# Changing the place of small pieces of work in a decoder trunk: gate rows, sample scores, norms, first blocks and a queue's order

## The reference, cut to what matters

```
mod    = c @ w_ada[l] + b_ada[l]                 # 2 layers x 12 blocks of 512 columns: shift, scale, gate
u      = x * (1 + scale(c)) + shift(c)
# layer 0
q, k, v, mq, mk, mv, og, ig, fg = split(u @ w_in_even)      # "ein": 3072 columns and 8 gate columns
A      = softmax(q k1 - alibi) v - lam * softmax(q k2 - alibi) v     # 4 differential heads, causal; samples: paged past too
M      = mlstm(mq, mk, mv, ig, fg)               # 4 heads; state C, n, m; normalised by max(|den|, exp(-m))
mix    = concat(rms(A) * gA, rms(M) * g * sigmoid(og))
x      = LayerNorm(ALPHA * x + (1 + gate(c)) * (mix @ w_out_even))   # "eout"
x      = LayerNorm(ALPHA * x + (1 + gate(c)) * swiglu(u'))           # ffn 0
# layer 1
xr, g  = u @ w_in_odd                             # "oinx", "oing"
xc     = conv4(xr);  r, i = sigmoid(xc @ w_a), sigmoid(xc @ w_x)     # "wax"
a      = exp(-8 r softplus(-lambda));  h_t = a h_(t-1) + sqrt(1 - a^2) i xc
x      = LayerNorm(ALPHA * x + (1 + gate(c)) * ((gelu(g) * h) @ w_out_odd))   # "oout"
x      = LayerNorm(ALPHA * x + (1 + gate(c)) * swiglu(u'))           # ffn 1
```

## Time and profile before

| | |
|---|---|
| median of 3 runs | 1556.14 us (1552.59 to 1557.97) |
| the profiled execution | 1546.92 us, of it the span 1545.3 us |
| PE busy | 1413.6 us, 91% |
| DVE, ACT, POOL busy | 775.5 us (50%), 529.4 us (34%), 319.1 us (21%) |
| mean bandwidth from and to HBM | 112 GB/s over the span |

### The profile page before, as it was taken

The page is one execution under the profiler, slowest core; times in us unless marked ns, Lnnn a source line. Parts: engine busy times, 40 slices in busy tenths (PEclk is TensorE's granted clock), DMA queues, the critical chain, the costliest instruction groups (busy, mean ns, idle before and its releaser), DMA issues.

```text
span 1545.3 us, 29474 instructions
## 1 busy us (share of the span) xinstructions
PE 1413.6 (91%) x12260; PEld 1353.9 (88%) x12260; DVE 775.5 (50%) x1179; ACT 529.4 (34%) x736; POOL 319.1 (21%) x303
## 2 busy tenths in 40 slices
PE   5799977788697999999999988988989999999996
PEld 4799966665597999999999988988989999999995
DVE  2633248764457633333334687788574333333256
ACT  0311143243323333212223345785433321222224
POOL 2000031021116500000002624634543000000054
PEclk9899988999898999999999999999999999999999
DMA  9522277666813122243322402221513224432211
GB/s 320 180 87 82 83 274 242 215 235 222 281 39 83 55 82 75 76 123 96 97 60 76 137 28 78 92 61 53 162 38 110 65 59 114 129 85 65 76 38 56
DMA packets 213505, 175.08 MB, mean 113 GB/s; under 512 B 9080, under 2 KB 183933, under 8 KB 213253
## 3 DMA queue, kind: packets, MB, share of 16 engines
q1 hardware_dynamic: 208448, 160.13, 33.7%
q0 software_dynamic: 4800, 13.23, 2.5%
q10 hardware_dynamic: 140, 0.09, 0.0%
HBM read 167.87 MB, written 5.63 MB: 112 GB/s over the span
## 4 chain that ended last, share of the span: by engine, by line
PE 53%; DVE 11%; ACT 3%; issue 2%; POOL 0%; ACTq 0%; DVEq 0%; POOLq 0%
PE ps L2647 44%; PE ps L2672 4%; PE ps L2656 3%; DVE gn L2100 2%; DVE wlo L1900 2%; DVE UL L2107 1%; ACT whi L1152 1%; DVE rstd L2073 1%; DVE xc L2221 1%; DVE xc L2255 0%; DVE xc L2256 0%; DVE tv L2065 0%; PE ps L2867 0%; ACT xT L1226 0%; DVE xT L2050 0%
## 5 line engine op out<-in xcount | busy, mean ns | idle before, releaser
L2647 PE MATMUL ps<-UH,whi 128*128 128x260 f32 x1840 | 372.8, 284 | 11.6 <-DVE wlo L1900 8.1
L2647 PE MATMUL ps<-UH,wlo 128*128 128x260 f32 x1840 | 372.6, 284 | 0.0
L2647 PE MATMUL ps<-UL,whi 128*128 128x260 f32 x1840 | 372.2, 284 | 0.0
L1152 ACT ACTIVATE whi<-raw 128x2048 fp32r<-128x2048 f32 (+3 forms) x104 | 178.0, 1712 | 433.2 <-PE ps L2647 396.7
L2647 PEld LDWEIGHTS ps<-UH,whi 128*128 128x128 f32 x1840 | 285.9, 190 | 12.6 <-issue 6.4
L2647 PEld LDWEIGHTS ps<-UH,wlo 128*128 128x128 f32 x1840 | 285.7, 190 | 0.0
L2647 PEld LDWEIGHTS ps<-UL,whi 128*128 128x128 f32 x1840 | 285.0, 190 | 0.0
L1900 DVE TENSOR_TENSOR wlo<-raw,whi 128x2048 fp32r<-128x2048 f32 (+3 forms) x104 | 224.4, 2158 | 79.1 <-ACT whi L1152 78.5
L2154 DVE TENSOR_TENSOR hb<-ps,silb 128x520 f32<-128x520 f32 x44 | 30.8, 700 | 267.4 <-PE ps L2647 247.3
L814 POOL COPY accS<-xT 128x520 f32<-128x520 f32 x4 | 2.5, 622 | 628.2 <-DVE xT L2032 628.2
L2647 PE MATMUL ps<-HH,whi 128*128 128x260 f32 x484 | 97.4, 283 | 0.0
(11 more groups left out here) (493 smaller groups left out, 2546.5 us busy)
## 6 DMA issues: line engine op xcount, KB each, us to landing
raw<-in_w_ada SPq DMA_DIRECT2D x96, 512.0 KB, 6.3
raw<-in_w_ffn_in SPq DMA_DIRECT2D x88, 512.0 KB, 5.0
raw<-in_w_in_even SPq DMA_DIRECT2D x24, 512.0 KB, 4.7
raw<-in_w_ffn_out SPq DMA_DIRECT2D x32, 384.0 KB, 4.0
raw<-in_w_ffn_out SPq DMA_DIRECT2D x32, 320.0 KB, 3.3
raw<-in_w_in_odd SPq DMA_DIRECT2D x20, 512.0 KB, 4.6
raw<-in_w_out_odd SPq DMA_DIRECT2D x16, 320.0 KB, 3.5
page<-in_cache_k POOLq DMA_DIRECT2D x16, 256.0 KB, 4.2
```

The lines of the kernel that those rows point to most:

```text
L1152: ins = nc.scalar.activation(whi[w % 2][:, 0:f], raw[c % NRAW][:, 0:f], ACT.Identity)
L2647: ins = T.matmul(ps(g)[:, hf, 0:HT], wt(k, m), x[:, k, hf], start=(k == 0 and wt is wh and x is xh), stop=(k == s.k - 1 and wt is wl_))
```

## The change: places of work, and orders in queues

Five places change. No matmul of a projection is added or removed.

1. The first four blocks are taken in the order 0, 2, 1, 3; the first chunk of `ein` is loaded between the pairs, and PE does the second pair between the fourth and the fifth k-slice of that chunk. The second pair's turns go to the second bank of the block's own PSUM group.
2. At the gate rows, blocks 4 and 5 are copied before DVE's running sums.
3. In the steps, the pieces for the samples move to later steps.
4. The two high and low halves for `eout` and the norms of heads 0 to 2 move into step 16. The mixing goes in the order `MIXED`, the sample columns of all eight tiles as one piece "S".
5. In the second mixer ACT copies `xrS` and frees the group; the GELUs of tiles 4 and 5 come earlier in ACT's queue, two low halves change their places in DVE's.

The diff follows, cut to its core, engine by engine. The plan and SP:

```diff
-PAST_AT, TURN_AT = {10: 0, 12: 1, 13: 2, 15: 3}, {11: 0, 13: 1, 14: 2, 16: 3}
+PAST_AT, TURN_AT = {11: 0, 12: 1, 14: 2, 15: 3}, {12: 0, 13: 1, 15: 2, 16: 3}
...
+FIRST_BLOCKS = (0, 2, 1, 3)
+MIXED = (0, 1, 2, "S", 4, 5, 6, 3, 7)
...
+    one(("mod", 0), ("mod", 1), ("sel", 0), ("sel", 1), ("mod", 2), ("mod", 3))
     stage("ein", 12, 8, 256, 2)
+    st["ada0"].chunks[4:] = [5, 6, 7, 8]
+    st["ein"].chunks[0] = st["ein"].c0 = 4
...
+                    if s.c0 == 0 and c == NRAW:
+                        load(st["ein"], 0)
```

POOL in the steps:

```diff
                     for e in range(2):
                         load_page(e, "cache_v", e)
+                if s_ == 9:
                     pool.wait_ge(n_new, 1)
...
-                if s_ == 8:
+                if s_ == 10:
                     pool.wait_ge(cgain_ready, 1)
...
-                if s_ in (11, 13, 14):
+                if s_ in (12, 13, 15):
                     p = TURN_AT[s_]
                     wait_filled(pool, use[("pv8", p)])
```

ACT, in the steps, then in the second mixer:

```diff
+                if s_ == 16:
+                    act.wait_ge(tokens_stored, 32)
+                    act.wait_ge(sample_stored, 48)
+                    hi(st["eout"].c0)
+                    hi(st["eout"].c0 + 1)
+                    link(nc.scalar.activation(sml[:, 12:13], epsc[:], ACT.Sqrt))
                 if quarter == 0 and 1 <= h <= H:
                     head_out(h - 1)
...
+                nc.scalar.activation(xrS[:, t].rearrange("p (a b) -> p a b", a=2), ps(g)[:, :, HALF:HT], ACT.Identity)
                 nc.scalar.activation(xc[:, t], pT(g), ACT.Identity, scale=OT[:, t, 35:36],
                                      bias=OT[:, t, 36:37]).then_inc(cv0, 1)
                 settled(act, cv0)
+                free(nc.scalar.activation(sml[0:1, 13:14], ps(g)[0:1, 0, 0:1], ACT.Identity), g)
...
+            gelu(0)
+            gelu(4)
+            gelu(5)
+            gelu(1)
+            gelu(2)
+            high_y(0)
```

DVE at the gate rows, in the steps, in the mixing, in `make_u0` and in the second mixer:

```diff
             link(v.tensor_scalar(rows[0:4, 0], rows[0:4, 0], 15.0, None, ALU.mult))
+            block_rows(FIRST)
+            block_rows(FIRST + 1)
+            block_select(FIRST)
...
+                if s_ == 16:
+                    lo(st["eout"].c0)
+                    wait_filled(dve, use[("pv8", 3)])
+                    lo(st["eout"].c0 + 1)
+                    dve.wait_ge(den_ready, H - 1)
+                    dve.wait_ge(expm_ready, 1)
+                    norm_floor(slice(0, 96))
...
-                if s_ == 0:
+                if s_ == 7:
                     own_scores()
-                if s_ == 3:
                     sample_gates()
-                if s_ == 4:
                     state_dots()
-                if s_ == 5:
+                if s_ == 8:
                     pack_states()
...
+            mixed(0)
+            dve.wait_ge(root_ready, 2)
+            v.reciprocal(R[96:128, 0:P], R[96:128, 0:P])
...
+                    if t == 4:
+                        low(3)
+                    if t % 4 == 0:
+                        first_scale_and_shift(t // 4)
                     if t == 2:
-                        lo(st["ein"].c0)
-                    if t == 5:
-                        lo(st["ein"].c0 + 1)
+                        lo(st["ein"].chunks[0])
...
                 low(KD - 1)
+                lo(st["ein"].chunks[1])
...
-                free(v.tensor_copy(xrS[:, t].rearrange("p (a b) -> p a b", a=2), ps(g)[:, :, HALF:HT]), g)
-                dve.wait_ge(freed[g % NGRP], g // NGRP + 1)
...
                 scan(t)
-                if t == 2:
+                if t == 0:
                     lo(p0 + 12)
```

PE in the mixing and in the first chunk of `ein` and `eout`:

```diff
-            for t in range(8):
+            for i, t in enumerate(MIXED):
                 g = use[("rb", t)]
+                if t == "S":
+                    pe.wait_ge(r_ready, 2)
...
+                ks = [t for t in MIXED if t != "S"] if mixer else list(range(s.k))
+                for i, k in enumerate(ks):
+                    if i == 4 and between is not None:
+                        between()
+                    pe.wait_ge(ready, max(4, i + 2) if mixer else n_ready + k + 1)
...
+                for d in (2, 3):
+                    block_products(d)
+                for d in (2, 3):
+                    block_turn(d)
...
-            gemm("ein", UH, UL, ulo_ready, 0)
+            gemm("ein", UH, UL, ulo_ready, 0, between=last_blocks)
```

More of the change, by code:

```diff
@@ L545, in weight_view @@
                 both = [a["w_ada"][l].rearrange("(e k p) (c m) -> c e p k m", e=2, p=P, m=512) for l in range(2)]
-                return [both[block_of(s, c) // 12][block_of(s, c) % 12][c % 2] for c in range(s.n)]
+                named = [FIRST_BLOCKS[d] if d < FIRST else d for d in range(NBLK)]
+                return [both[named[block_of(s, c)] // 12][named[block_of(s, c)] % 12][c % 2] for c in range(s.n)]
             if n == "ein":
@@ L628, in _ @@
                 turn = s.c0 > 0 and is_ada(s.c0 - 1) != is_ada(s.c0)
-                peel = min(s.n, NRAW) if s.c0 == 0 or turn else 0
+                peel = NRAW + (s.name == "ein") if s.c0 == 0 or turn else 0
                 if is_ada(s.c0) and s.c0 > 0:
                     peel = s.n
-                for c in range(peel):
+                for c in range(s.name == "ein", peel):
                     load(s, c)
@@ L949, in middle_act @@
             settled(act, zeroed)
-            for tb in range(1, 4):
-                token_rows(tb)
+            token_rows(2)
+            token_rows(3)
             for tb in range(4):
@@ L1451, in _, with gelu @@
             s = st["oing"]
-            for t in range(KR):
-                if t == 6:
-                    hi(p0 + 15)
-                if t == 8:
-                    hi(p0 + 16)
+            def gelu(t):
                 g = s.groups[t // 2][t % 2]
@@ L1469, in _ @@
                     act.wait_ge(freed[g % NGRP], g // NGRP + 1)
-                if t >= 1:
-                    high_y(t - 1)
-            high_y(KR - 1)
+            gelu(0)
[4 more added lines that the diff above has]
+            high_y(0)
+            gelu(3)
+            high_y(1)
+            gelu(6)
+            high_y(2)
+            gelu(7)
+            hi(p0 + 15)
+            for t in range(3, 6):
+                high_y(t)
+            gelu(8)
+            high_y(6)
+            high_y(7)
+            gelu(9)
+            hi(p0 + 16)
+            high_y(8)
+            high_y(9)
             s = st["oout"]
@@ L1870, in middle_dve @@
+            dve.wait_ge(mix_hi, 4)
+            v.tensor_tensor(samples(ML[:]), ms, samples(MH[:].bitcast(F32)), ALU.subtract).then_inc(mix_lo, 1)
+            settled(dve, mix_lo)
+            for i in range(5, 9):
+                mixed(i)
+                low_mixed(i - 1)
+            low_mixed(8)
             for j in range(2):
@@ L1959, in block_rows @@
                 wait_filled(dve, g)
+                if d in (2, 3):
+                    v.tensor_copy(modrow[:, d % 2], ps(g)[:, 0, 0:P]).then_inc(rows_copied, 1)
+                    settled(dve, rows_copied)
+                    return
                 free(v.tensor_copy(modrow[:, d % 2], ps(g)[:, 0, 0:P]), g)
@@ L1992, in _, with first_scale_and_shift @@
             setup_dve()
-            for d in range(FIRST):
-                block_rows(d)
-                if d >= 1:
-                    block_select(d - 1)
-            block_select(FIRST - 1)
-            scale_and_shift(0)
+            def first_scale_and_shift(i):
+                for d in (2 * i, 2 * i + 1):
+                    block_rows(d)
+                for d in (2 * i, 2 * i + 1):
+                    block_select(d)
+                t = slice(4 * i, 4 * i + 4)
+                link(v.tensor_scalar(G9[:, 0, t], part(0, 1)[:, t], 1.0, None, ALU.add))
+                link(v.tensor_copy(B9[:, 0, t], part(0, 0)[:, t]))
             def make_u0():
@@ L2665, in first_k_ordered @@
                 pe.wait_ge(lo_done, split_index[s.c0] + 1)
-                for k in range(s.k):
-                    pe.wait_ge(ready, n_ready + k + 1)
+                mixer = s.name == "eout"
+                ks = [t for t in MIXED if t != "S"] if mixer else list(range(s.k))
[3 more added lines that the diff above has]
+                    pe.wait_ge(ready, max(4, i + 2) if mixer else n_ready + k + 1)
                     for m in range(s.uses):
@@ L2823, in block_turn @@
             def block_turn(d):
+                gm = use[("mod", d)]
+                if d in (2, 3):
+                    pe.wait_ge(rows_copied, d - 1)
+                    T.matmul(ps(gm)[:, 1, 0:36], modrow[:, d % 2], cn[:, C_ADA:C_ADA + 36], start=True, stop=True).then_inc(turned, 1)
+                    return
                 g = use[("sel", d)]
                 begin(g)
-                gm = use[("mod", d)]
                 pe.wait_ge(freed[gm % NGRP], gm // NGRP + 1)
```

243 lines of the change are left out of this document (137 added, 106 removed).

## The result

The changed kernel takes 1546.36 us (median of 13 runs, 1544.73 to 1549.52) against 1556.14 us for the kernel before in the same job (13 runs, 1549.53 to 1565.36): a ratio of 0.9933 [0.9913, 0.9953], or 9.8 us. It is faster, as forecast, but by 9.8 instead of 24.2 us. The profiled execution took 1548.51 us.

A forecast was written before the change was run, and what follows sets the result against it. TensorE was busy 1413.6 of 1545.3 us, so only about 132 us could be won from. Terms -7 + 0 - 2.5 - 7.7 - 7 = -24.2, taken off the median 1556.14, gave 1532 us; range 1519 to 1548.

The forecast's parts named there:

- A: Start, first blocks in pairs: the first projection's chunk 1 begins at 56.3 instead of 64.28; taken as 7 us, bounds 4 to 8.5.
- B: Gate rows: the 7.02 us wait for VectorE becomes a wait for DMA; gain 0, from -1.5 to +1.5 us.
- C: The 18 steps: later sample pieces bring early steps forward, little is left at the loop's end; -2.5 us, from -6 to +2.
- The sign that the prediction had named: Loop's end: the forecast is wrong if the loop's last steps come later than today.
- 4.9 us of moved work at nothing: Steps 7 to 9: 4.9 us of moved work costs nothing in VectorE's pauses; 9.4 us falls to about 4.5.
- rival 3: Steps 7 to 14: pushed-together sample pieces each show TensorE a wait of 4.5 us; slower, 1561 us; chance 0.04.
- the pages' "about 10 us": Loop's end: last value pages, asked for after step 14, needed after step 15; issue some 4 us, landing 5.9.
- ACT's halves in an idle time of 7.82 us: Ahead of the last head's outputs: the idle time holds two high halves of 1.91 us and a table load, if chunks landed.
- Rival 2: Loop's end: shared DMA engines make last pages and projection chunks late, holding the last head; about 1540 us; chance 0.14.
- D: Norms and mixing: from last sums to output projection 13.8 us instead of 21.5; gain 7.7, bounds 5 to 10.
- E: Second mixer: xrS waits of 7.7 us and a low-half wait of 4.83 go; -7 us, from -3 to -10.
- rival 1: Second mixer: waits only change hands within VectorE's queue, gain there 1 us; total 1538 us; chance 0.17.

The follow-up runs named there:

- the second pair: pages_early against old_steps, which differ by the moved steps and both keep the halves ahead of the last head: 1552.39 and 1543.77 us.
- the first experiment: The kernel before, unedited, profiled a second time: 1558.41 us, 0.9993 of before, profiled span 1556.9.
- combined_again: combined run once more without edit, beside combined_moved: 1538.44 us, 0.9895 of before.
- combined_moved: Against combined: sample pieces in the change's later steps, third pair of value pages used in step 13: 1546.64 us, 0.9957 of before.
- combined: Changed kernel with sample pieces, pages, state products in before's steps, halves behind the last head, second mixer's projection low half first: 1535.24 us, 0.9858 of before.
- pages_early: Changed kernel with the third pair of value pages used in step 13 instead of 14, the fourth asked for a step earlier: 1552.39 us, 0.9962 of before.
- old_steps: Changed kernel with all sample pieces, pages and state products in before's steps, the rest kept: 1543.77 us, 0.9901 of before.

## Why the prediction was right in direction and wrong in size

**A and B** came out by their mechanism: 5.9 of 7 us at chunk 1, less by DVE's later tiles (1.4) and the slow clock behind PE's new pause (0.7), and at the gate rows the wait for DVE turned into one for a transfer. Together -4.7 at step 0, or -6.5 against the profile from which the forecast was read.

**C is the step that failed**, in both halves: in the table above 8.9 of the 14.2 us by which -10.0 misses -24.2 are C's. The sign that the prediction had named came: the loop ends later than before (last sums at 425.96, 415.78 and 424.29 in the two profiles of before).

*Up to step 13* the prediction said that pieces taken out of the front make Sb earlier, which they do (unit 9 comes 96.9 us after the first Sb, against 102.4 in the quick profile and 107.4 in the other), and that 3.7 us of this would be kept at step 13. It was not shown to be kept: unit 13 comes after 151.0 us, against 144.0 and 153.8. PE's idle time over the steps is 32.4 us after and 31.3 to 31.7 before. The waits of the earlier trace rows were not removed: after, the Sb rows among PE's waits are these (who, whom, us, times, longest):

```profile
PE ps L2501 <- DVE Sb L1591: 9.1, 6, 2.4
...
PE ps L2596 <- DVE Sb L1591: 3.5, 1, 3.5
```

The prediction had priced 4.9 us of moved work at nothing, to lie in DVE's pauses. Its sum there is wrong as well: of the 7.7 us it charged 2.8, so 9.4 falls to 6.6; it took off the 4.9 instead and wrote 4.5. The experiments say that the moves as a whole are worth less than nothing: 8.2 us worse with the end repaired, 8.6 in the second pair. Not quite half of that is idle time in the last units; the rest is clock, and a profile of one execution cannot tell a lower clock that the order causes from one by chance (the first experiment). The clocks of the other runs point the same way, 0.958 to 0.966 in the six runs of combined_again and 0.953 to 0.960 in the eleven of combined_moved. The medians show the sum, and the windows that it is lost behind unit 12. There PE's waits in combined_moved are for `pvrow` (4.6 us, 2.6 in combined), for Sb (2.0, 0.5) and for `proj` of the past values (1.6, none). That points at the values over the past, which are pushed together there much as rival 3 described, at a smaller price; no run moves them alone, and which of the pieces costs it stays open.

*At the end* the prediction took -2.5 for all of C, with +2 as the worst, and this stretch alone measured +7.2. It had seen both mechanisms, and judged that both would just fit. The term that failed in the changed kernel is the pages' "about 10 us" between asking and need. They are asked for from 397.21 on, and PE would have taken the first at 401.49 (403.33 less its wait), 4.3 us later; the four take 4.2, 4.9, 6.5 and 7.9 us to land. PE stands 5.15 us for them, and 1.6 us go to the slow clock behind the wait. The other term, ACT's halves in an idle time of 7.82 us "if the two chunks have landed by then", failed too, since they had not: the first chunk is asked for at 399.19 and split at 408.33. But in the changed kernel this cost nothing, because the head itself came later still; it costs 3.4 to 5.1 us at the end where the pages come early (pages_early, old_steps). Pages and chunks are asked for in the same 5 us, 3 MB in all: the halves of the two chunks take 8.7 us to land (median of four), against 6.7 in the kernel before and 5.2 and 6.0 in the two kernels with early pages. Rival 2 described this lateness. That its price of about 8 us (pages, head, and a part of D) lies near the 7.2 is luck: the pages and the clock behind them cost nearly all of it instead of 2 to 3 us, the head behind ACT cost nothing, and D lost nothing. The rule of the Trainium skill cited beside C, that transfers of all issuing engines share the same 16 DMA engines ("DMA: Bandwidth & Descriptors", section "Issuing engines are not separate DMA queues"), agrees with these landing times.

**D** was right: the projection starts 13.24 us after the sums, for 13.8. That is -9.75 against the second profile of before and -8.3 against the first, for -7.7. But part of it was only carried forward: with the halves back behind the head, and both causes out, the projection starts 16.0 us after the sums, so 5.5 to 7 us come from the norms and the mixing's order and the rest from the halves.

**E** had the right mechanism and a mis-sized term. xrS and the moved low half did what they should, the new wait for the next low half came at 4.12 for 5.2. "The output projection meets the next low half about 8 us early at best" was the wrong term: PE came early and stood 7.00 us, since that low half lies behind five YL pieces which took 8.26 us together, against 5.64 for five before. Moving it ahead of them gave 4.0 us in the medians; -3.9 had been E's yield (-4.4, and +0.5 behind it). This is rival 1 for the last of E's chunks.

**The frame.** Taking the 24.2 us off the median was right. Where the time goes could not be read from the quick profile of before: by it the steps would have lost 9.8 us, by the other one they won 0.8.

The best kernel here is combined: 1535.24 and 1538.44 us in two jobs, 24 and 15 us under the kernel before on the same chip. It keeps A, B, E, the norms and the mixing's new order, and gives up all of C's moves and D's early halves; the first low half of the second output projection stands first.

## What to carry to other kernels

Work that is moved into an idle time of an in-order engine must have its inputs there *before* that idle time begins, and the row to check is the issue of its transfer, not the length of the pause; when two groups of transfers are asked for within a few microseconds, count their bytes together. Moving pieces between steps whose waits all end in one engine's queue changes where the waits stand; compare the sum of PE's idle time over all steps, not the start of one. When two causes each suffice, undoing one shows nothing: undo both before you drop a theory. And read the idle time behind moved work too: where the engine still waits after it (4.37 us here), the moved work held nothing.

## What was not expected of the hardware

The granted clock of TensorE in the same stretch of the same program differs from run to run: in one unit of the steps 0.95 and 0.75 (PE busy 6.57 and 9.49 us for the same 99 matmuls, idle 4.25 and 4.23), over the steps 0.93 and 0.85, which is 11 us of 162. And the low half of a YL tile took 1.65 us in the middle of the second mixer (8.26 for five), while one of the first mixer's tiles took 0.70.
